# A decoder step on one core: the first layer's decode attention placed between the tiles of its projection

## What is computed

```
for g, (window, dil) in ((128,1), (512,4), (2048,16)):
    q, k, v = h @ w_in[g]                       # prompt rows and decode rows
    decode: keys  = cache_a_win{g}[b, every dil-th row, 0], 128 of them, + the new key
            logits = q . key / 8 + bias(dil * distance)
    prompt: keys among the 256 rows, dist % dil == 0, dist <= window
out = sum over g of softmax over all three groups' keys together, times the values
x = x + out @ w_out ; x = x + mlp(rmsnorm(x))   # mlp: relu(h @ up)^2 @ down
outputs: the caches shifted by one row with the new row put in (the "copies"), the new prompt rows
```

## Time and profile before

| | us |
|---|---|
| timed runs | 1934.84, 1943.52, 1977.62 (median 1943.52) |
| the profiled execution's own time | 1929.27 |
| its span (first to last instruction) | 1927.6 |
| mean granted clock of TensorE | 0.88 of full |
| busy: TensorE 1710.1, weight loads 1436.9, VectorE 568.7, POOL 317.7, ScalarE 226.9 | |

### The profile page before, as it was taken

How to read it: one execution, slowest core, us unless ns; L and a number is a source line. 1 busy time by engine, 2 the same in 40 slices (tenths; PEclk the granted TensorE clock), 3 DMA queues, 4 the chain that set the end, 5 groups by cost and what they waited for, 6 DMA issues and landing times.

```text
span 1927.6 us, 23264 instructions
## 1 busy us (share of the span) xinstructions
PE 1710.1 (89%) x8890; PEld 1436.9 (75%) x8890; DVE 568.7 (30%) x1449; ACT 226.9 (12%) x687; POOL 317.7 (16%) x379
## 2 busy tenths in 40 slices
PE   5999999699998994999999997999987645899996
PEld 4878787588898984888888886877754423688885
DVE  3111111255212012455544443513444500322002
ACT  0010001244111000000000000114522200000000
POOL 0000000124110101323233331002213342000000
PEclk8799999799655566899999999998998877899998
DMA  5599999900233528789988896891015664575440
GB/s 170 206 377 391 391 393 387 355 1 1 73 101 96 164 102 249 247 326 339 342 327 322 332 349 234 273 391 56 1 58 179 203 207 147 214 282 182 145 152 23
DMA packets 180926, 423.43 MB, mean 220 GB/s; under 512 B 13208, under 2 KB 154824, under 8 KB 178008
## 3 DMA queue, kind: packets, MB, share of 16 engines
q1 hardware_dynamic: 147992, 327.49, 46.1%
q0 software_dynamic: 25712, 84.25, 13.7%
q10 hardware_dynamic: 7120, 10.32, 1.7%
HBM read 413.88 MB, written 192.48 MB: 315 GB/s over the span
## 4 chain that ended last, share of the span: by engine, by line
PE 80%; DVE 6%; issue 4%; DMA 4%; POOLq 2%; ACT 1%; ACTq 1%; POOL 1%; SPq 0%; DVEq 0%
PE bank L587 21%; PE bank L744 6%; PE bank L757 6%; PE bank L828 6%; PE bank L722 4%; PE bank L701 4%; PE bank L848 4%; PE bank L675 4%; PE bank L775 3%; PE bank L782 3%; PE bank L778 3%; DMA a_win_sample<-oT 3%; PE bank L905 2%; PE bank L630 2%; POOLq L369 1%
## 5 line engine op out<-in xcount | busy, mean ns | idle before, releaser
L587 PE MATMUL bank<-hT,wring 128*128 128x264 f32 x1664 | 393.0, 393 | 1.1 <-DMA wring<-a_w_in 0.8
L587 PEld LDWEIGHTS bank<-hT,wring 128*128 128x128 f32 x1664 | 319.1, 194 | 56.2 <-DMA wring<-a_w_in 1.3
L517 POOL DMA_INDIRECT cring<-cache_b_kv,keyrow x128 | 128.5, 1004 | 246.0 <-PE bank L782 215.6
L675 PE MATMUL bank<-ident,cring 128*128 128x128 f32 x512 | 103.1, 353 | 27.6 <-DVE bias L345 14.6
L744 PE MATMUL bank<-hT,wring 128*128 128x264 f32 x512 | 116.9, 393 | 8.2 <-DVE hT L1096 8.2
L828 PE MATMUL bank<-area,wring 128*128 128x264 f32 x512 | 119.2, 386 | 0.4 <-issue 0.4
L744 PEld LDWEIGHTS bank<-hT,wring 128*128 128x128 f32 x512 | 99.1, 194 | 26.0 <-issue 8.6
L757 PE MATMUL bank<-area,wring 128*128 128x264 f32 x512 | 114.2, 386 | 1.4 <-DVE area L1274 1.4
L675 PEld LDWEIGHTS bank<-ident,cring 128*128 128x128 f32 x512 | 82.5, 196 | 43.5 <-issue 21.4
L757 PEld LDWEIGHTS bank<-area,wring 128*128 128x128 f32 x512 | 97.2, 190 | 18.4 <-DVE area L1272 1.8
L828 PEld LDWEIGHTS bank<-area,wring 128*128 128x128 f32 x512 | 97.2, 190 | 16.9 <-issue 0.8
(11 more groups left out here) (276 smaller groups left out, 2119.5 us busy)
## 6 DMA issues: line engine op xcount, KB each, us to landing
a_win_sample<-cache_a_win SPq DMA_DIRECT2D x64, 2047.0 KB, 17.6
wring<-a_w_in SPq DMA_DIRECT2D x36, 1024.0 KB, 16.5
wring<-mlp_w_up SPq DMA_DIRECT2D x32, 1024.0 KB, 5.4
wring<-mlp_w_down SPq DMA_DIRECT2D x32, 1024.0 KB, 5.1
a_win_sample<-cache_a_win SPq DMA_DIRECT2D x16, 2044.0 KB, 13.4
cring<-cache_a_win POOLq DMA_DIRECT2D x48, 512.0 KB, 5.7
cring<-cache_b_kv POOLq DMA_DIRECT2D x128, 128.0 KB, 3.1
cring<-cache_b_kv SPq DMA_DIRECT2D x128, 128.0 KB, 3.0
```

Of the source, the lines that this page charges most:

```text
L517: pool.indirect_dma_start(out=land[:, s4, u * 512:(u + 1) * 512], out_offset=None, in_=rows, in_offset=bass.IndirectOffsetOnAxis(ap=keyrow ...
L587: mm = pe.matmul(bk[half][0:width, 0:R], wring[:, blk % NW, c, half * P:half * P + width], rhs[:, c, :], start=(c == 0), stop=(c == DC - 1))
L675: mm = pe.transpose(bk[2 + n % 2][:, i * P:(i + 1) * P], src[i], ident[:, :])
```

## The change

- The tiles of the projection come in another order: all 24 query tiles, then the 24 key tiles, then the 24 value tiles (kind = i // 24, g = i // 8 % 3).
- The decode attention is done between these tiles, in two sets st of four requests. A unit x = (st, g) has 128 past keys of four requests, loaded by POOL as 16 transfers (`load_kd`) in quarters of 32 partitions; VectorE turns them in place in blocks of 32 x 32 (`dve.transpose`, 24 of 128 x 1024, at the tiles of KT_AT); TensorE multiplies them as the moving side with queries as weights, 32 columns (of which 16 count) for each request in its own column group (`scores_d` at the tiles of KD_AT). Queries are laid out by 32 small VectorE copies at tile 23 (qx).
- Logits lie with four requests by heads on the partitions and the keys along the row (LAd), so the softmax is one reduce, one exp and one scaling for each set, at tiles 50 to 53. The new key's logits are 24 matmuls of one column at tile 49, from products made at tile 47 (qkx). Probabilities are turned (tile 52), values are the moving side (`values_d`, six units at the tiles of VD_AT), and VectorE picks each head's columns with a mask and adds (tiles 61 and 70). The new values are added inside the prompt's attention (units 6 to 9), and pv1 is put into oT before the output projection.
- ScalarE stores rown before the prompt's rows, each under its own semaphore (rown_stored, k_stored[g], rows_stored), and waits for the one that it needs. The wait of VectorE and POOL for all stores ahead of the prompt's attention is gone; ScalarE waits for rown_stored there. POOL's first mixes wait for pnd_ready, pd_turned and pvd_done.
- The copies: with blocks 2 to 11, 18 paced by the units of the first prompt attention, with blocks 40 to 71, 16 paced by the units of the second, the other 20 from block 87 on.
- The slots of cring are now loaded for the second layer alone; the old decode code and its tables (bias_s, nbias, c_mnew) go.

```diff
...
+KD_AT = (24, 25, 35, 38, 45, 48)
+VD_AT = (55, 56, 60, 62, 66, 69)
...
+        if k == B_AIN:
+            j = j // 4 % 3 * 12 + j // 12 * 4 + j % 4
...
-        if i >= 4 and shifts:
+        if (2 <= i < 12 or B_UP0 <= i < B_BIN or i >= B_UP1) and shifts:
             d, s = shifts.pop(0)
             sp.dma_start(d, s).then_inc(S["copies_done"], 16)
+        if i == B_AOUT + 3:
+            for k in range(18):
+                sp.wait_ge(S["pv_done"], 1 + 5 * k // 3)
+                d, s = shifts.pop(0)
+                sp.dma_start(d, s).then_inc(S["copies_done"], 16)
+        if i == B_BOUT + 3:
...
+                sp.wait_ge(S["pv_done"], 2 * H + 1 + 2 * k)
...
+    def load_kd(u):
+        if u == 1:
+            pool.wait_ge(S["biasd_done"], 1)
+        if u >= 2:
+            pool.wait_ge(S["kd_used"], u - 1)
+        st, g = u // 3, u % 3
+        for j in range(4):
+            src = t[f"cache_a_win{g}"][0, 4 * st + j].rearrange("(k r) a h d -> k r a (h d)", r=DIL[g][1])[:, 0, 0, :]
+            for a in range(4):
+                pool.dma_start(land8[32 * a:32 * a + 32, 4 * (u % 2) + j].rearrange("p (k n) -> p k n", k=4),
+                               src[:, 256 * a:256 * a + 256].rearrange("(k p) n -> p k n", k=4)).then_inc(d_landed[u % 2], 16)
+    def load_vd(y):
+        if y < 2:
+            pool.wait_ge(S["kd_used"], 5 + y)
+        else:
+            pool.wait_ge(S["pvd_done"], y - 1)
+        st, g = y // 3, y % 3
+        for j in range(4):
+            src = t[f"cache_a_win{g}"][0, 4 * st + j].rearrange("(k r) a h d -> k r a (h d)", r=DIL[g][1])[:, 0, 1, :]
+            pool.dma_start(land8[:, 4 * (y % 2) + j], src).then_inc(d_landed[y % 2], 16)
...
+    load_kd(0)
+    pool.wait_ge(S["gemm_done"], DC)
+    nc.gpsimd.memset(qx_f, 0.0).then_inc(S["qx_zero"], 1)
+    nc.gpsimd.memset(qkx_f, 0.0).then_inc(S["qx_zero"], 1)
+    for u in range(1, 6):
+        load_kd(u)
+    for y in range(6):
+        load_vd(y)
+    pool.wait_ge(S["bias_evac"], 9)
+    pool.wait_ge(S["pnd_ready"], 1)
+    pool.wait_ge(S["pd_turned"], 2)
...
+        if h == 1:
+            pool.wait_ge(S["pvd_done"], 5)
...
-    for i in range(2, 2 * NB):
-        load(i)
...
+    def scores_d(x):
+        st, k = x // 3, x % 3
+        if x == 0:
+            pe.wait_ge(S["qx_ready"], 1)
+            pe.wait_ge(S["biasd_read"], 1)
+        pe.wait_ge(S["kd_turned"], 4 * (x + 1))
+        if x >= 2:
+            pe.wait_ge(S["logd_read"], x - 1)
+        for hd in range(8):
+            for j in range(4):
+                o = ((k * 4 + j) * 8 + hd) * H
+                mm = pe.matmul(bk[4 + x % 2][32 * j:32 * j + 32, 0:P], qx_f[:, st, o:o + 32], kd[:, 4 * (x % 2) + j, :, hd, :],
+                               start=(hd == 0), stop=(hd == 7))
+        mm.then_inc(S["kd_used"], 1)
+    def values_d(y):
+        st, k = y // 3, y % 3
+        pe.wait_ge(d_landed[y % 2], unit_landed(6 + y))
+        pe.wait_ge(S["ptd_ready"], st + 1)
+        if y == 3:
+            pe.wait_ge(S["od_read"], 1)
+        for x in range(2):
+            for j in range(4):
+                mm = pe.matmul(bk[6 + x][32 * j:32 * j + 32, :], PTd[:, st, k, 32 * j:32 * j + 32], land8[:, 4 * (y % 2) + j, 512 * x:512 * x + 512],
+                               start=(k == 0), stop=(k == NG - 1))
+        mm.then_inc(S["pvd_done"], 1)
...
-            g, kind, c = i // 24, i // 8 % 3, i % 8
+            kind, g, c = i // 24, i // 8 % 3, i % 8
             held = None if kind == 0 else (i, kT[:, g, c, :] if kind == 1 else vtmp[:, i % 2, :])
+            if i == 4:
+                pe.wait_ge(S["tab_ready"], 5)
+                for q in range(4):
+                    mm = pe.matmul(bk[4 + q][:, 0:NLQ], tabrep[32 * q:32 * q + 32].rearrange("p j h -> p (j h)"), oh[32 * q:32 * q + 32, 1022:1022 + NLQ],
+                                   start=True, stop=True)
+                mm.then_inc(S["biasd_done"], 1)
+            if i in KD_AT:
+                scores_d(KD_AT.index(i))
+            if i == 49:
+                pe.wait_ge(S["qkx_ready"], 1)
+                pe.wait_ge(S["logd_read"], 5)
+                for st in range(2):
+                    for k in range(NG):
+                        for j in range(4):
+                            o = (k * NB + 4 * st + j) * H
+                            mm = pe.matmul(bk[4][32 * j:32 * j + 32, NG * st + k:NG * st + k + 1], qkx_f[:, o:o + 32], ones[:, 0:1], start=True, stop=True)
+                mm.then_inc(S["newlog_done"], 1)
+            if i == 52:
+                for st in range(2):
+                    pe.wait_ge(S["pd_ready"], st + 1)
+                    for k in range(NG):
+                        mm = pe.transpose(bk[4 + st][:, k * P:(k + 1) * P], LAd[:, st, k * P:(k + 1) * P], ident[:, :])
+                    mm.then_inc(S["pd_turned"], 1)
+            if i == 57:
+                pe.wait_ge(S["pnd_ready"], 1)
+                for st in range(2):
+                    for k in range(NG):
+                        mm = pe.matmul(bk[4 + st][:, k * P:(k + 1) * P], ones[:, :], pnd[:, NG * st + k, :], start=True, stop=True)
+                mm.then_inc(S["pnd_done"], 1)
+            if i in VD_AT:
+                values_d(VD_AT.index(i))
...
+    pe.wait_ge(S["od_ready"], 2)
+    for st in range(2):
+        mm = pe.transpose(bk[6 + st][0:HD, 0:P], od[:, st, :], ident[:, :])
+    mm.then_inc(S["od_turned"], 1)
...
-    turn(0)
-    for n in range(n_sel0):
-        if n + 1 < n_sel0:
-            turn(n + 1)
-        it, _, (g, x) = groups[n]
-        b, sq = it[1], squares(n)
-        if g == 0 and x == 0 and b >= 2:
-            pe.wait_ge(S["qk_read"], b - 1)
-        for i in range(4):
-            c = 4 * x + i
-            mm = pe.matmul(bk[4 + b % 2][:, g * H + 2 * c:g * H + 2 * c + 2], sq[:, i * P:(i + 1) * P], qbd[:, g, b, c, :],
-                           start=True, stop=True)
-        mm.then_inc(S["sq_used"], 1)
...
+    KT_AT = (12, 13, 14, 15, 16, 17, 18, 19, 31, 32, 33, 34, 35, 36, 37, 37, 42, 43, 44, 44, 45, 46, 47, 47)
...
+        if i == 5:
+            dve.wait_ge(S["biasd_done"], 1)
+            for q in range(4):
+                ins = dve.tensor_copy(LAd[:, :, NLQ * q:NLQ * (q + 1)], bk[4 + q][:, 0:NLQ].unsqueeze(1).broadcast_to([P, 2, NLQ]))
+            ins.then_inc(S["biasd_read"], 1)
+        if i in KT_AT:
+            for n in range(24):
+                if KT_AT[n] == i:
+                    dve.wait_ge(d_landed[n // 4 % 2], unit_landed(n // 4))
+                    dve.transpose(land8[:, n % 8, :], land8[:, n % 8, :]).then_inc(S["kd_turned"], 1)
+        if i == 23:
+            dve.wait_ge(S["qx_zero"], 2)
+            dve.wait_ge(S["gemm_evac"], E_AIN + 24)
+            for a in range(4):
+                for hh in range(4):
+                    for x in range(2):
+                        src = qT[64 * (hh % 2) + 32 * x:64 * (hh % 2) + 32 * x + 32, :, 2 * a + hh // 2, SEQ:R]
+                        ins = dve.tensor_copy(qx[32 * a:32 * a + 32, :, :, :, 2 * hh + x, 4 * a + hh], src.rearrange("p g (t b) -> p t g b", t=2))
+            ins.then_inc(S["qx_ready"], 1)
+        if i - 1 in KD_AT:
+            x = KD_AT.index(i - 1)
+            dve.wait_ge(S["kd_used"], x + 1)
+            if x == 0:
+                dve.wait_ge(S["biasd_read"], 1)
+            L = LAd[:, x // 3, x % 3 * P:(x % 3 + 1) * P]
+            dve.scalar_tensor_tensor(L, bk[4 + x % 2][:, 0:P], SCALE, L, ALU.mult, ALU.add).then_inc(S["logd_read"], 1)
+        if i == 47:
+            dve.wait_ge(S["gemm_evac"], E_AIN + 48)
+            for e in range(2):
+                for k in range(NG):
+                    ins = dve.tensor_tensor(qkx[64 * e:64 * e + 64, k, :, :, e], qT[64 * e:64 * e + 64, k, :, SEQ:R].rearrange("p c b -> p b c"),
+                                            kT[64 * e:64 * e + 64, k, :, SEQ:R].rearrange("p c b -> p b c"), ALU.mult)
+            ins.then_inc(S["qkx_ready"], 1)
+        if i == 50:
+            dve.wait_ge(S["newlog_done"], 1)
+            for st in range(2):
+                L = LAd[:, st, NG * P:NG * P + NG]
+                ins = dve.scalar_tensor_tensor(L, bk[4][:, NG * st:NG * st + NG], SCALE, L, ALU.mult, ALU.add)
+            ins.then_inc(S["logd_read"], 1)
+            dve.wait_ge(S["logd_read"], 7)
+            for st in range(2):
+                ins = dve.tensor_reduce(mxd[:, st:st + 1], LAd[:, st, 0:NG * P + NG], AX.X, ALU.max, negate=True)
+            ins.then_inc(S["maxd_ready"], 1)
+        if i == 51:
+            dve.wait_ge(S["expd_done"], 2)
+            link(dve.reciprocal(rcd, smd))
+            for st in range(2):
+                L = LAd[:, st, 0:NG * P + NG]
+                dve.tensor_scalar(L, L, rcd[:, st:st + 1], None, ALU.mult).then_inc(S["pd_ready"], 1)
+        if i == 53:
+            for st in range(2):
+                dve.wait_ge(S["pd_turned"], st + 1)
```

(54 more changed lines are left out.)

281 lines of the change are left out of this document (89 added, 192 removed).

## The result

| | predicted | before | after |
|---|---|---|---|
| timed runs, us | 1735 (1712 to 1766) | 1934.84, 1943.52, 1977.62 | 1753.01, 1778.10, 1781.82 |
| median, us | 1735 | 1943.52 | 1778.1 |
| the profiled execution, us | 1725.5 | 1929.27 | 1781.82 (span 1780.1) |
| mean granted clock of it | | 0.88 | 0.904 |

After over before is 0.9105, 95% interval 0.8813 to 0.9396: faster, by less than predicted, and the median lies 12 us above the range.

What follows compares the result with a forecast made beforehand. The prediction took TensorE to bound the whole kernel, with the decode attention at half clock; gains of 241.6 us less costs of 37.8 gave 1725.5 us profiled, 1735 timed, range 1712 to 1766.

Steps and rivals of the forecast that it cites:

- the sum's last: Whole kernel: from the profiled 1929.3 us, less 203.8, to 1725.5; 0.3% to 0.7% more for timed runs gives 1735.
- its own terms: Bounds behind the range: costs 30 to 60 us, stores 8 to 16, boundary 0 to 13, and 0.4% between profile and median.
- The start: Ahead of the projection: the dropped bias matmul gains 0.4 us.
- What goes: Decode attention between prompt attention and output projection goes, leaving 0.8 us before the output projection: gain 212.7 us.
- The row stores: Projection: three ScalarE store stalls go, as decode rows are sent first and no copies run beside them: gain 16.2 us.
- The boundary: Projection's last tile to first turn of probabilities: shorter store landing and earlier POOL mixes leave about 6.5 us, gain 10.8.
- What TensorE gets: Decode products added between projection tiles: scores 2.2 us a unit, values 1.83, with new keys, turns and bias 28.9 us together.
- Between them: Going into and out of column groups at 14 places in the projection: 5 us lost, between 2.4 and 8.1.
- VectorE: Beside the projection: query copies at tile 23 delay TensorE 1.4 us (0 to 4); turns, masked reduces and softmax 1 us.
- Attention extras: Inside the prompt's attention: six small products and three sums on VectorE before units 6 to 9 cost 1.5 us.
- POOL and the queues: Projection: key units need 14.5 us of the 27 available, weights have 21 us of slack; no stall.
- The moved copies: Copies beside the two prompt attentions and in the last MLP cost nothing; 2 to 5 us if they slowed weights there.

Runs made afterwards that it cites:

- run 3: Changed kernel plus filler products nobody reads ahead of the waits of the first six units of each prompt attention: median 1740.4 us, ratio 0.8965.
- run 7: Kernel before, plus filler products at the entries and in the next five units of its two prompt attentions: median 1941.0 us, ratio 0.9952.
- run 5: Changed kernel with fillers in both prompt attentions, POOL's first key loads behind inputs and constants, query copies spread over tiles 17 to 23: median 1730.6 us.
- run 1: Changed kernel unaltered, timed again: median 1752.0 us (1740.0 to 1808.4), ratio 0.9013 to the kernel before.
- run 4: Changed kernel with POOL's 16 key loads of the first unit waiting until inputs and constants have landed: median 1749.5 us, ratio 0.889.
- run 8: Changed kernel with the old row-store rule alone (prompt rows first, ScalarE waits for both), copies as changed: one execution, 1753.0 us.
- run 11: Changed kernel with 8 of the 32 score products of each unit: a unit takes 0.57 us between two tiles instead of 1.88.
- run 9: Changed kernel with the copies issued as before, one per weight block from block 4, row stores as changed: median 1811.9 us, ratio 0.9291.
- run 2: Changed kernel with the 16 copies paced by the second prompt attention moved to the second projection's blocks: median 1767.6 us, ratio 0.8977.

## Why the prediction was wrong

**The step that failed is the sum's last**: that every stage that the change doesn't touch keeps the length of the profiled execution of before, and that 0.3% to 0.7% on it makes the timed one (range: 0.4%). The profiled execution, at 1929.27 us, was at the bottom of what before does: its second attention has a mean clock of 0.92, with the lower level for the first 19 us alone.

```profile
1299.30:1411.70 112.40, 111.97 (x669) 81.05 (x668) 42.87 (x294) 55.31 (x257) 25.64 (x31) 0.92 0.09 35
```

The kernel before took 1930 to 2014 us in later executions, with medians of 1947 to 1964, 1% to 2% above it. The prediction read the clock of the decode attention and the 0.97 of the first prompt attention, and didn't ask what these stages take when the clock falls otherwise. A pair of units of the second attention takes 12.4 us at the lower level and 6.8 at the upper, by the timeline of after, so 88 us more of lower clock (107.4 against 19) are 40 us; the table has +39.8. The Trainium skill, page "TensorE: Matmul & The Clock Gate", section "Seeing it yourself", has seen the gate stuck at a quarter for over 50 us and calls such events of a trace unreliable; here the level is a half for 107.4 us, and the durations of the products agree with it. With the clock held in both kernels (runs 3 and 7) the change is worth 1941.0 - 1740.4 = 200.6 us; the sum had 203.8. These are two chips, and the fillers differ by the 32 that stand in before's wait for the stores. On one chip, run 5 is 210.4 us below run 7; without its own two further edits (15.0 us at the start, 2.3 at the query copies) that is 193.

**What was luck**: the median of the three timed executions, 1778.1, lies above the range, but that of six more executions of the same program (run 1) is 1752.0 and lies inside. The range was also narrower than its own terms: added plainly, they reach from 1718 to 1783, and how they became 1712 to 1762 is not written down.

**The start** was costed at a gain of 0.4. It lost 6.5: POOL now issues 16 key loads in the first microseconds, and the input that TensorE waits for lands 5.6 us later. The prediction looked at the queues from tile 4 on and not at what the same loads do ahead of the first instruction. Run 4 shows it.

**What goes** (212.7): right. The output projection starts 4.6 us after the attention's end, and its eight tiles take 28.7 us, 28.5 predicted.

**The row stores** (16.2): right in size, since no such stall is left, half right in cause. Both reasons were named; run 8 shows that the copies' absence does most and the order little in the projection (1.3 us of stall come back with the old rule alone).

**The boundary** (10.8): right; 6.3 us.

**What TensorE gets**: scores 1.88 a unit (2.2), values 1.86 (1.83; the trace of after has x16 in 1.92, less the overlap of ends). **Between them**: 0.13 us a place, under the low end of 0.17, by run 11. The Trainium skill, page "TensorEngine Tiling (Array Packing)", section Key Properties, has a change of tiling mode drain TensorE; here that drain is inside the 0.13.

**VectorE**: the 32 copies took 0.197 us each, not 0.13, and the stall was 2.3 against 1.4; with the slower scores behind it, which the sum had at nothing, 3.8, just inside the bound of 4. The turns, the masked sums and the softmax stalled nothing: TensorE's only waits in the projection are these 2.3 us and 1.3 for weights.

**Attention extras** (1.5): nothing to be seen, by runs 5 and 7.

**POOL and the queues**: right that no one waits for the keys. "No stall" for the weights missed 1.3 us. And the keys fit only because the copies had left: run 9, with the copies where they were, is 58 us longer there.

**The moved copies** (nothing): right, by runs 2, 5 and 7; the last MLP, which keeps 20 of them, takes 116.8 and 114.2 us in its two halves by the chain of waits, against 116.9 and 114.2.

What stays open: why a low stretch lasts 22 us in one execution and 107 in another of the same program; and what each of the two entries does alone, since the fillers were never put at one only.

## What to carry to other kernels

Before a sum is made on a profiled execution, look for stages where TensorE is busy and its clock is at the lower level, and ask whether they could be otherwise in the next execution; a timed spread of some per cent is the sign. A short wait of TensorE at the entry of a stage of small products can be filled with products that nobody reads: 14 of them here took 1752 us with 68 us of spread to 1716 with 5, together with the later key loads and the spread copies; the key loads alone had left a spread of 64 us (run 4). When work is put beside a stage, its transfers come along: count the bytes of that stage's queues before and after, and for the first microseconds too.
